# First attention of a two-part network: the value products of two units in one stretch, and four slots for the turned weights

## The reference, cut to what matters

```python
def attend_block(args):
    q, k, v, m = args
    s_loc = jnp.einsum("bqhgd,bkhd->bhgqk", q, k).astype(F32) * scale
    s_loc = jnp.where(m, s_loc, -jnp.inf)
    s_ctx = jnp.einsum("bqhgd,bchd->bhgqc", q, kc).astype(F32) * scale
    p = softmax_with_sink(jnp.concatenate([s_loc, s_ctx], axis=-1), sink_b).astype(v.dtype)
    return (jnp.einsum("bhgqk,bkhd->bqhgd", p[..., :3 * BLOCK], v)
            + jnp.einsum("bhgqc,bchd->bqhgd", p[..., 3 * BLOCK:], vc))
```

## Time and profile before

| | |
|---|---|
| median of 3 runs | 4016.49 us (4014.26 to 4023.72) |
| the profiled execution | 4022.94 us, its span 4021.2 us |
| mean granted TensorE clock | 0.979 |
| busy over the span | PE 94%, PEld 56%, DVE 44%, ACT 30%, POOL 23% |
| the stage of the change | about 266 to 543 us of the span |

### The profile page before, as it was taken

One profiled execution on the slowest core, in us unless ns is written; L12 is line 12 of the kernel. 1 busy time (PEld: TensorE's weight loads), 2 busy tenths in 40 slices (PEclk: granted clock), 3 DMA queues, 4 the chain that ended last, 5 costly groups with the idle time before them and its releaser, 6 DMA issues. The chain is left out here.

```text
span 4021.2 us, 70289 instructions
## 1 busy us (share of the span) xinstructions
PE 3793.9 (94%) x29530; PEld 2270.1 (56%) x29530; DVE 1774.6 (44%) x3668; ACT 1214.7 (30%) x2214; POOL 926.4 (23%) x586
## 2 busy tenths in 40 slices
PE   8999999989989999999898998997999989988998
PEld 3458854445556666644355446444544468888643
DVE  3346643232134444442455237216544456575422
ACT  1137731112246556511311027112200222222124
POOL 0000023410000000053232210422122137675442
PEclk9999999999999999999999999998999999999999
DMA  6000033241322010030422021101232221212300
GB/s 230 21 22 2 2 106 115 84 105 69 110 80 67 25 48 25 5 111 0 162 89 79 0 85 63 42 0 41 87 128 84 79 98 45 71 45 92 112 10 38
DMA packets 176993, 269.28 MB, mean 67 GB/s; under 512 B 50869, under 2 KB 96421, under 8 KB 176551
## 3 DMA queue, kind: packets, MB, share of 16 engines
q1 hardware_dynamic: 176680, 264.78, 18.9%
HBM read 197.72 MB, written 66.76 MB: 66 GB/s over the span
## 5 line engine op out<-in xcount | busy, mean ns | idle before, releaser
L2188 DVE TENSOR_SCALAR_CACHE_REDUCE la_s<-psum 128x512 f32<-128x512 f32 (+1 forms) x384 | 210.2, 597 | 192.3 <-PE psum L2254 192.1
L2161 ACT ACTIVATE la_pT<-psum 128x512 f32<-128x512 f32 x320 | 172.9, 593 | 216.9 <-PE psum L2264 216.9
L966 POOL TENSOR_TENSOR lg_seven_s<-other_columns 128x512 f32<-128x512 f32 x4 | 5.1, 1264 | 891.7 <-POOLq L112 871.2
L2152 ACT ACTIVATE la_s<-la_s,la_negm 128x1280 f32<-128x1280 f32 x128 | 174.6, 1364 | 18.5 <-DVE la_negm L2197 14.8
L2264 PE MATMUL psum<-ident,la_s 128*128 128x128 f32 x1280 | 166.2, 277 | 0.1
L2264 PEld LDWEIGHTS psum<-ident,la_s 128*128 128x128 f32 x1280 | 139.0, 140 | 40.7 <-issue 35.2
L4706 PE MATMUL psum<-rs_inverse,rs_Z 64*64 64x64 f32 x2560 | 155.7, 223 | 4.4 <-DVE rs_Z L4558 3.3
L987 PE MATMUL psum<-room,x_rows 128*128 128x512 f32 x320 | 147.0, 603 | 4.7 <-POOL x_rows L966 4.7
L4704 PE MATMUL psum<-rs_Z,rs_inverse 64*64 64x64 f32 x2048 | 135.0, 224 | 16.6 <-DVE rs_Z L4558 16.1
L2248 PE MATMUL psum<-la_kT,la_qT 64*128 64x512 f32 (+1 forms) x672 | 143.1, 544 | 7.3 <-DVE la_s L2188 7.3
L966 POOL TENSOR_TENSOR wg_seven_s<-other_columns 128x512 f32<-128x512 f32 x5 | 6.3, 1265 | 591.6 <-POOLq L112 544.4
(11 more groups left out here) (745 smaller groups left out, 8222.0 us busy)
## 6 DMA issues: line engine op xcount, KB each, us to landing
later_slot<-in_ada_w_dram SPq DMA_DIRECT2D x16, 1024.0 KB
rwkv_raw<-x_rows SPq DMA_DIRECT2D x64, 256.0 KB, 2.0
room<-rwkv_raw SPq DMA_DIRECT2D x32, 512.0 KB, 4.5
room<-in_even_w_in_dram SPq DMA_DIRECT2D x6, 2048.0 KB, 11.5
room<-in_odd_w_in_dram SPq DMA_DIRECT2D x6, 2048.0 KB, 12.8
ada_slots<-in_ada_w_dram SPq DMA_DIRECT2D x8, 1024.0 KB, 9.7
rwkv_raw<-room SPq DMA_DIRECT2D x16, 512.0 KB, 2.6
latent_v<-lp_v SPq DMA_DIRECT2D x10, 512.0 KB, 2.7
```

The source lines that it names most:

```text
L2152: act.activation(s_sb[:, g % 2, j, :], s_sb[:, g % 2, j, :], ACT.Exp, bias=negm[:, g % 2, j:j + 1], accum_out=total[:, g % 2, j:j + 1]).th ...
L2161: act.activation(pT[:, h, at * BANK:(at + 1) * BANK], pT_banks[turn], ACT.Copy).then_inc(pT_moved[turn], 1)
L2188: dve.tensor_scalar(s_sb[:, g % 2, j, cols], s_banks[j][:, 0:cols.stop - cols.start], SCALE, NEG, ALU.mult, ALU.max, accum_out=smax[:, g % ...
```

## The change

In `window_attend`, TensorE computes no values in even rounds. In odd rounds from 3 to 81 it computes those of two units, `values(u - 3)` and `values(u - 2)`, one directly behind the other. The values of an even unit thus come one round later than before, those of an odd unit in the same round. So that the turned weights live long enough, `pT` has four slots in place of two (10 KB more in each partition, only in this stage), and the waits on `pv_made` of `copies` and `fifth` go back four units.

```diff
+    SLOTS = 4
...
-        s_sb, pT = sb("s", [P, 2, 2, A_KEYS_X]), sb("pT", [P, 2, 2, 5, P])
+        s_sb, pT = sb("s", [P, 2, 2, A_KEYS_X]), sb("pT", [P, SLOTS, 2, 5, P])
...
-                        if u >= 2 and b == 0:
-                            act.wait_ge(pv_made, u - 1)
-                        act.activation(pT[:, u % 2, b, :, :].rearrange("p t q -> p (t q)")[:, 0:n], pT_banks[b][:, 0:n], ACT.Copy).then_inc(pT_moved, 1)
+                        if u >= SLOTS and b == 0:
+                            act.wait_ge(pv_made, u - SLOTS + 1)
+                        act.activation(pT[:, u % SLOTS, b, :, :].rearrange("p t q -> p (t q)")[:, 0:n], pT_banks[b][:, 0:n], ACT.Copy).then_inc(pT_moved, 1)
...
-                    if u >= 2:
-                        dve.wait_ge(pv_made, u - 1)
-                    dve.tensor_copy(pT[:, u % 2, :, 4, :], fifth_bank[:, 0:2 * P].rearrange("p (b q) -> p b q", b=2)).then_inc(fifth_moved, 1)
+                    if u >= SLOTS:
+                        dve.wait_ge(pv_made, u - SLOTS + 1)
+                    dve.tensor_copy(pT[:, u % SLOTS, :, 4, :], fifth_bank[:, 0:2 * P].rearrange("p (b q) -> p b q", b=2)).then_inc(fifth_moved, 1)
...
-                    if 2 <= u <= U + 1:
+                    if u % 2 and 3 <= u <= U + 1:
+                        values(u - 3)
                         values(u - 2)
```

More of the change, by code:

```diff
@@ L922, in values @@
                             rows, g = slice(b * A_DIM, (b + 1) * A_DIM), (p // 4) * 2 + b
-                            last = pe.matmul(o_bank[rows, (p % 4) * P:(p % 4 + 1) * P], v[:, k, g * A_DIM:(g + 1) * A_DIM], pT[:, u % 2, b, n, :],
+                            last = pe.matmul(o_bank[rows, (p % 4) * P:(p % 4 + 1) * P], v[:, k, g * A_DIM:(g + 1) * A_DIM], pT[:, u % SLOTS, b, n, :],
                                              start=(n == 0), stop=(n == len(tiles(u)) - 1))
```

## The result

The changed kernel takes 4037.65 us (median of 4 runs, 4035.69 to 4039.5) against 4016.9 us before (4 runs): a ratio of 1.0043, 95% interval 1.0031 to 1.0055. It is slower, by 20.8 us between the medians; the forecast was 4033.6, in a range of 4026 to 4041.

A forecast was written before the change was run, and what follows sets the result against it. TensorE was taken to set the pace, with a scores-to-maxima loop just shorter than its work. Stage terms 11.3 + 2.5 + 1.6 + 2.2 - 0.5 gave +17.1 us on a 4016.5 median: 4033.6 us, range 4026 to 4041.

The forecast's parts named there:

- The loop: Even rounds, five key tiles: scores, VectorE's reads, next scores through one PSUM place take 3.28 us, against TensorE's own 2.64.
- the context: Rounds 3 to 15, two key tiles: even rounds 1.83 us, odd 2.41, together 27.85 instead of 25.64: +2.2 us.
- The added stretch: Odd rounds: a second unit's values directly behind the first add 1.09 us with five key tiles, making 4.97 us.
- twice 1.09 + 0.05: Sign expected in the changed profile: length in us of the odd rounds' value stretches of 40 records.
- The sum: Whole stage: 11.3 for five key tiles, 2.5 tile 2, 1.6 tile 9, 2.2 context, less 0.5: +17.1 us.
- The end: Last transposes of the stage: two waits for ScalarE covered by the longer last round, some -0.5 us, an estimate.
- case C: Loop longer than read, VectorE's 0.24 us slack failing or ScalarE copies late: +8 us more, 4041.4 us; chance 8%.
- The price of a change of form: TensorE's entry into the values, one fewer per two rounds: 0.15 us saved per pair if nothing else hinders.
- A: No wait appears in even rounds; about 39 pairs each save 0.15 us: -5.9 us, 4010.6 us; chance 6%.
- B: TensorE's new idle times also slow its clock in four stretches: +7 us more, 4040.6 us; chance 7%.
- D: Even rounds' loss partly hidden, say by VectorE starting earlier: 0.15 to 0.2 us less per pair, 4026 to 4028; chance 9%.

The follow-up runs named there:

- the halved read: Changed kernel with VectorE reading only the first half of each head's scores: 4031.22 us in one run, stage 290.9 us.
- the two splits: Kernel before, moving only part of even units' values into odd rounds: two key tiles, 4025.74 us (1.0008); all but the first, 4033.62 us (1.0030).
- the halved kernels: Changed kernel and kernel before, each with VectorE's read and ScalarE's exponentials halved: 4021.2 us (1.0001) and 4025.15 us (1.0009).

## Why the prediction was right

**The loop, 3.28 us.** Right, to the rounding: 3.28 measured in the rounds with five key tiles, 2.80 with four, 1.83 in the context. Shown by the halved read, which brought the even round down to TensorE's own work, and by the two splits: an even round of 3.44 us loses nothing, one that wants 3.00 takes 3.28.

**The added stretch, 1.09 us.** Right: the odd rounds take 4.97. There is no gap between the two units' values, and the 40 records' loads last 2.16 us. From the start of the stretch to the next scores it is 2.33 us (394.17 - 391.84), which is 1.24 + 1.09, as in the sum; the "twice 1.09 + 0.05" among the signs of the prediction, 2.23, doesn't agree with its own sum and was 0.1 short.

**The sum, by stretches.** These are the starts of scores on PEld that bound them in the changed kernel, with the start of the next stage at the end:

```profile
301.86 0.96 PEld L887 LDWEIGHTS psum<-window_kT,window_qT 64*128 64x128 f32 x12 [0.17 <-issue]
...
336.44 1.16 PEld L887 LDWEIGHTS psum<-window_kT,window_qT 64*128 64x128 f32 x12 [0.17 <-issue]
...
526.13 0.73 PEld L887 LDWEIGHTS psum<-window_kT,window_qT 64*128 64x128 f32 x8 [0.17 <-issue]
...
562.66 0.30 PEld L989 LDWEIGHTS psum<-first_weights,columns 128*128 128x128 f32 x2 [1.62 <-issue]
```

The stretches take 35.51, 34.58, 189.69 and 36.53 us; before, by the earlier trace rows and the stage's bounds, 32.86, 32.11, 178.38 and 35.28. The differences are +2.65, +2.47, +11.31 and +1.25, against +2.2, +2.5, +11.3 and +1.1 (1.6 less 0.5) in the prediction, so 17.7 against 17.1. The one term that was clearly short is the context, by 0.45 us: most odd rounds take 2.46 us and not 2.41, and the first of them 2.68. I had taken the mean of all rounds, 1.97, for an odd one; before, odd rounds there took 1.89 to 1.94, and the mean held three longer even ones of 2.14 to 2.19. The added 0.44 would have made 2.36 out of 1.92. The rest is in the transposes: their four loads take 0.53 us in these rounds and 0.42 before, most likely a wait for the second head's exponential. The end gave back 0.3 us where I had estimated 0.5.

**From the profiled execution to the median.** I added 17.1 to a median of three runs and got 4033.6; the difference measured in more runs is 17.6, and the first comparison, from four runs each, showed 20.8. The time alone says little: 4037.65 lies as near to case C's 4041.4 as to the forecast, and the range of 15 us took in both. It is the distances of 3.28 and 4.97 us and the stage's 17.7 us that speak for the mechanism.

**The price of a change of form.** I took 0.15 us out of a bound of 0.09 to 0.26; the halved kernels show 0.15. The Trainium skill (TensorEngine Tiling (Array Packing), Key Properties) says that a change of tiling mode drains TensorE. The 0.17 us without a load that PEld shows at an entry agree with that, though no row shows the drain itself. By its rule alone the sign would have been wrong: the wait that the values had covered cost 0.64 us a pair, four times what one entry less could save. The Trainium skill's rule that groups should rotate through PSUM banks (Perfetto Trace Analysis, Optimizing Tensor Performance, Matmuls) gave the right sign; the 0.57 us that PE waits in each even round agree with it.

**The rivals.** A fell: the even rounds are 3.28, not 2.70. B fell: the granted clock stayed at 1.00 from 330 to 520 us in spite of 0.57 us of idleness in every second round. (The 0.37 us that it quotes as of rows 6 is PE's wait at 301.78, shown above.) C didn't come, although the slack was as small as I had worked out, 0.24 us ahead of VectorE's read in the rounds with the sums. D fell: VectorE starts 1.40 us after the scores begin when it was idle for 2.37 us (387.33 - 385.93), and 1.41 when it was idle for 0.24 (390.61 - 389.20).

## What to carry to other kernels

An engine without a gap can still stand in a loop that is almost as long as its own work. Before moving work away from between a producer and the next use of the same buffer, add up the loop (here 1.40 + 1.82 + 0.06 = 3.28 us) and compare it with what is left in the round (2.64): here moving was free down to the loop's length and cost in full below it. Saving an entry into another form of the array is worth 0.15 us here, which is little beside any wait.

## What was unexpected of the hardware

Nothing in the clock or the engines' durations; the distances repeat to 0.01 us or so from round to round. What I had not expected is that with two slots the tiles with few keys lose 8 us while those with five lose next to nothing, and that with four key tiles VectorE's read and ScalarE's work hold TensorE for equally long: a pair takes 6.91 us in the changed kernel, 6.90 with VectorE's read halved, and 6.48 with the exponentials halved too. Easing VectorE alone gained nothing; easing ScalarE alone wasn't run.
